# Routing gates scattered into DRAM by accumulating indirect DMAs, searches packed into the first half of the u pass

## The reference

```
q = (xc @ w_q).reshape(TOKEN_CHUNK, PEER_HEADS, 2, PEER_HALF)
s = jnp.einsum('thpd,hpnd->thpn', q, keys)
top_s, top_i = lax.top_k(s, 16)                       # of 128 keys, in each half
cand = top_s[:, :, 0, :, None] + top_s[:, :, 1, None, :]
best_s, best_j = lax.top_k(cand.reshape(..., 256), 16)
expert = i1 * 128 + i2                                # 16384 experts
g = jax.nn.softmax(best_s, axis=-1)
act = gelu(einsum('thk,td->thk', u_tab[expert], xc)) * g
out = einsum('thk,thkd->td', act, v_tab[expert])
```

## Time and profile before

| | |
|---|---|
| median of three runs | 2736.47 us |
| the profiled execution's own time | 2744.57 us |
| its span, first to last instruction | 2742.8 us |
| PE busy | 2465.3 us (90%) |
| DVE busy | 2131.3 us (78%) |
| ACT busy | 1234.8 us (45%) |
| POOL busy | 571.3 us (21%) |
| DMA, mean over the span | 254 GB/s |

### The profile page before, as it was taken

The page is one execution under the profiler, slowest core; times in us unless marked ns, Lnnn a source line. Parts: engine busy times, 40 slices in busy tenths (PEclk is TensorE's granted clock), DMA queues, the critical chain, the costliest instruction groups (busy, mean ns, idle before and its releaser), DMA issues.

```text
span 2742.8 us, 36197 instructions
## 1 busy us (share of the span) xinstructions
PE 2465.3 (90%) x10956; PEld 1938.4 (71%) x10956; DVE 2131.3 (78%) x3891; ACT 1234.8 (45%) x2704; POOL 571.3 (21%) x408
## 2 busy tenths in 40 slices
PE   4987888999899787899999999998878999999996
PEld 3767766666456576777777777776756888878885
DVE  4877613666388855889999999989688888888888
ACT  2332043444312142267777787777433333333333
POOL 2013104422032320011111111112122323232221
PEclk9999999999999899999999999999988999999998
DMA  6646651112032325478888888888899999999996
GB/s 275 217 163 253 255 218 62 62 62 86 23 117 101 146 78 217 136 263 309 322 299 319 298 319 309 305 304 313 318 387 347 381 382 388 384 368 380 389 382 237
DMA packets 223810, 697.60 MB, mean 254 GB/s; under 512 B 15840, under 2 KB 111456, under 8 KB 181472
## 3 DMA queue, kind: packets, MB, share of 16 engines
q1 hardware_dynamic: 165984, 367.25, 37.2%
q0 software_dynamic: 37632, 270.55, 26.0%
q10 hardware_dynamic: 20096, 58.72, 5.6%
HBM read 614.67 MB, written 81.79 MB: 254 GB/s over the span
## 4 chain that ended last, share of the span: by engine, by line
PE 42%; DVE 32%; DVEq 9%; DMA 8%; issue 5%; ACT 3%; SPq 1%; ACTq 1%; POOL 0%; PEldq 0%; PEld 0%
PE ps L866 21%; PE ps L557 7%; DVE g_acc L1787 5%; DVEq L1799 4%; PE ps L542 4%; DVE rows L1778 4%; DVE arena L1454 3%; DMA act_in<-act_scratch 3%; DVE hot L1741 2%; PE ps L569 2%; DMA arena<-in_weights 2%; DVE cand L1397 1%; PE ps L905 1%; DMA rows<-in_rows,pick_e 1%; DMA ring<-in_weights 1%
## 5 line engine op out<-in xcount | busy, mean ns | idle before, releaser
L1999 POOL DMA_INDIRECT rows<-in_rows,pick_e x256 | 333.4, 1302 | 1350.1 <-DVE g_acc L1787 1188.6
L1245 ACT CAST t_hi<-raw 128x1024 fp32r<-128x1024 f32 x256 | 268.8, 1050 | 545.0 <-PE ps L866 528.1
L866 PE MATMUL ps<-t_hi,c_hi 128*128 128x512 f32 x1024 | 407.4, 398 | 37.9 <-DVE t_lo L1859 33.0
L866 PE MATMUL ps<-n_hi,t_hi 128*128 128x512 f32 x1024 | 413.6, 404 | 26.4 <-DVE t_lo L1804 25.3
L866 PE MATMUL ps<-t_lo,c_hi 128*128 128x512 f32 x1024 | 404.4, 395 | 0.0
L866 PE MATMUL ps<-t_hi,c_lo 128*128 128x512 f32 x1024 | 404.1, 395 | 0.0
L866 PE MATMUL ps<-n_hi,t_lo 128*128 128x512 f32 x1024 | 401.2, 392 | 0.0
L866 PE MATMUL ps<-n_lo,t_hi 128*128 128x512 f32 x1024 | 401.0, 392 | 0.0
L1787 DVE SCALAR_TENSOR_TENSOR g_acc<-rows,small,g_acc 128x1024 f32<-128x1024 f32 x254 | 326.3, 1285 | 34.9 <-issue 9.1
L1934 POOL TENSOR_TENSOR w_lo<-ring,w_hi 128x1024 fp32r<-128x1024 f32 x76 | 189.4, 2498 | 667.2 <-ACT w_hi L998 559.9
L866 PEld LDWEIGHTS ps<-t_hi,c_hi 128*128 128x128 f32 x1024 | 196.2, 192 | 85.3 <-issue 44.5
(11 more groups left out here) (198 smaller groups left out, 4188.4 us busy)
## 6 DMA issues: line engine op xcount, KB each, us to landing
raw<-in_table SPq DMA_DIRECT2D x256, 512.0 KB, 7.2
ring<-in_weights SPq DMA_DIRECT2D x44, 2048.0 KB, 8.2
act_scratch<-act_out SPq DMA_DIRECT2D x128, 256.0 KB, 3.5
gate_scratch<-staged ACTq DMA_DIRECT2D x16, 2048.0 KB, 9.7
act_in<-act_scratch SPq DMA_DIRECT2D x128, 256.0 KB, 10.6
gate_in<-gate_scratch SPq DMA_DIRECT2D x32, 1024.0 KB, 15.6
arena<-in_weights ACTq DMA_DIRECT2D x24, 1024.0 KB, 9.4
arena<-in_weights SPq DMA_DIRECT2D x2, 2048.0 KB, 21.2
```

The lines of the kernel that those rows point to most:

```text
L866: last = mm(out, a, b_, start=start and x == 0, stop=stop and x == len(pairs) - 1, skip_group_check=True)
L1245: copy(t_hi[:, t % 2, :], raw[:, t % 4, :]).then_inc(hi_ready, 1)
L1999: G.indirect_dma_start(rows[:, j % 4, :], None, rows_in, bass.IndirectOffsetOnAxis(ap=pick_e[:, j:j + 1], axis=0)).then_inc(row_in[j % 4], 16)
```

## The change

The gate array becomes a DRAM array of cells (one float for each expert and token), laid out so that a tile's 128 x 512 gates are contiguous. SP clears it in the trunk of group 1 by 32 DMAs of 1 MB from a zeroed buffer. After every two searches DVE computes the cell numbers and the softmax weights of 2 x 16 picks for 128 tokens (`place_pair`, `weigh_pair`; ACT does the exp between them), and POOL issues 32 indirect DMAs, 128 single floats each, which add the weights into the cells: 512 in all. The one-hot steps on DVE, ACT and PE, the turned blocks and the 2 MB stores are gone. The v pass loads 256 KB of gates a tile in rows of 2 KB.

The searches all stand in u tiles 0 to 63, half a search a tile; no slots stand there. The slots start at tile 64: two a tile, but one in every fourth, to tile 127 (112 slots, 116 before); in the v pass one a tile and a second one in every eighth (144, 140 before). The v pass of DVE and ACT is written out instead of looped.

```diff
-        gate_dram = scratch("gate_scratch", QUARTERS, P, P, STAGE)
+        gate_cells = scratch("gate_scratch", P * P * SEQS[1], 1)
+        gate_dram = gate_cells.rearrange("(k p t) a -> k p (t a)", p=P, t=SEQS[1])
+        gate_zero = gate_cells.rearrange("(c p m n) a -> c p m (n a)", c=ZEROS, p=P, n=2 * P)
...
         def slots_of(k):
-            if k < 16 or P - 4 <= k < P:
+            if k < DENSE:
                 return ()
-            if k < 4 * CROWDED:
-                return (k - 16,)
...
+            if k < P:
+                j = 2 * (k - DENSE) - (k - DENSE) // 4
+                return (j,) if k % 4 == 3 else (j, j + 1)
+            j = k - 16 + (k - P + 4) // 8
+            return (j, j + 1) if k % 8 == 3 else (j,)
...
         def search_of(k):
-            if k < 4 * SEARCH_BODIES - 2:
+            if k < DENSE:
                 return k // 2, (0, 1) if k % 2 == 0 else (2, 3)
...
+                def clear(c):
+                    sp.dma_start(gate_zero[c], score_in[:, 1].rearrange("p a n -> p (a n)").unsqueeze(1).broadcast_to(
+                        (P, P * P * SEQS[1] // (ZEROS * P * 2 * P), 2 * P))).then_inc(zeroed, 16)
...
             store_act(P - 1)
+            for x in range(4):
+                sp.wait_ge(scattered[x], 16 * TOPK * HEADS)
+            for t in range(4):
+                load_gate(0, t)
...
-            def gate_step(s, parity, taken):
-                pe.wait_ge(sel_copied, taken)
-                pe.wait_ge(hot1_ready, s + 1)
-                pe.wait_ge(hot2g_ready, s + 1)
-                after(pe, g_copied, s - 1)
-                for x in range(4):
-                    last = mm(ps[:, 2 + parity, x * P:(x + 1) * P], hot1[:, parity, x, :], hot2g[:, parity, x, :],
-                              start=True, stop=True)
-                last.then_inc(g_done, 1)
...
+            def place_pair(p):
+                o, n, b = 32 * (p % 2), 32 * p, 2 * (p % 2)
+                keys1, keys2, v = (sel[:, x, o:o + 32] for x in range(3))
+                stt(out=keys1, in0=keys2, scalar=float(P), in1=keys1, op0=ALU.mult, op1=ALU.add)
+                V.tensor_copy(gsum[:, 0:2], v.rearrange("p (h k) -> p h k", k=TOPK)[:, :, 0])
+                dve.drain()
+                tt(v.rearrange("p (h k) -> p h k", k=TOPK), v.rearrange("p (h k) -> p h k", k=TOPK),
+                   gsum[:, 0:2].unsqueeze(2).broadcast_to((P, 2, TOPK)), ALU.subtract).then_inc(pair_shifted, 1)
+                for x in range(2):
+                    ts(cell[:, n + TOPK * x:n + TOPK * (x + 1)], keys1[:, TOPK * x:TOPK * (x + 1)], float(SEQS[1]),
+                       token[:, b + x:b + x + 1], ALU.mult, ALU.add)
...
+            def scatter(s):
+                b = s // TOPK % 4
+                if s % (2 * TOPK) == 0:
+                    pool.wait_ge(pair_ready, s // (2 * TOPK) + 1)
+                if s % TOPK == 0:
+                    after(pool, scattered[b], 16 * TOPK * (s // (4 * TOPK)))
+                G.indirect_dma_start(gate_cells, bass.IndirectOffsetOnAxis(ap=cell[:, s:s + 1], axis=0),
+                                     cell_g[:, s:s + 1], None, compute_op=ALU.add).then_inc(scattered[b], 16)
...
             for k in range(2 * P):
                 for j in slots_of(k):
                     if j + AHEAD < SLOTS:
                         gather(j + AHEAD)
-
-
+                known = 2 * TOPK * sum(pair_of(x) is not None for x in range(min(k, P)))
+                pace = 5 if k < DENSE else 4 if k % 4 == 0 else 3
+                while sent < known and (pace > 0 or k == P - 1):
+                    scatter(sent)
+                    sent += 1
+                    pace -= 1
```

More of the change, by code:

```diff
@@ L375, in load @@
                     load_unit(weights[UNITS_ADA + n], (b + n) % 2)
+                    if g and n == 2:
+                        sp.wait_ge(zero_ready, 1)
+                        for c in range(4):
+                            clear(c)
+                    if g and n in (9, 10):
+                        for c in range(2 * n - 2, 2 * n):
+                            clear(c)
                 if g == 0:
@@ L463, in _ @@
                 load_tile(k + 4)
[L464 to L471, removed]
-                        sp.wait_ge(gates_stored[half], 16 * QUARTERS // 2)
-                    load_gates(0, 0)
+                for x in range(2, SEARCHES):
+                    if starts(x - 1) == k:
+                        load_scores(sp, False, x)
                 if k == P // 2:
@@ L508, in _ @@
                         step(i, t, half)
-                    load_gates(i + 2, half)
             for t in range(4):
@@ L1807, in _ @@
             for k in range(P):
-                i, t = k // 4, k % 4
-                block = (i + 1 - SEARCH_BODIES) // 8 + 2 if (i + 1 - SEARCH_BODIES) % 8 == 0 else None
-                if block is not None and t == 0:
-                    shift_block(block % 2, 1)
-                for s in steps_of(k):
-                    hot_keys(s)
                 lower_tile(k + 1)
@@ L1844, in finish_gathered, with turn @@
                 tt(y, y, f_x1a[:, x, :], ALU.add).then_inc(y_ready, 1)
-            def turn(i, t, half, static=None, last=False):
-                if static is not None:
-                    slots = slots_of(static)
-                    use_slot(slots[0])
-                else:
-                    dve.wait_ge(row_in[t], 16 * i + 16 * (P // 4 + 1))
-                    V.tensor_tensor_reduce(out=rows[:, t, 0:D], in0=rows[:, t, 0:D], in1=x_tok[:, 1, :], scale=1.0,
-                                           scalar=0.0, op0=ALU.mult, op1=ALU.add, accum_out=dot[:, t:t + 1]
-                                           ).then_inc(dotted, 1)
+            def turn(i, t, last=False):
+                slots = slots_of(P + 4 * i + t)
+                use_slot(slots[0])
                 if not (last and t == 3):
@@ L2005, in _ @@
                 gather(j)
+            sent = 0
             for k in range(2 * P):
```

274 lines of the change are left out of this document (85 added, 189 removed).

## The result

The changed kernel takes 3056.64 us (median of four runs, 3051.4 to 3058.72) against 2737.36 us in the four runs of the kernel before beside them: a ratio of 1.1163, 95% interval 1.1144 to 1.1183. The forecast was 2761 us, from 2660 to 2880. The direction was right, the size was not: +319 us instead of +24, outside the range. The profiled execution has a span of 3056.9 us, 314.1 more than the 2742.8 of before.

A forecast was written before the change was run, and what follows sets the result against it. The prediction took DVE, closely followed by PE, to bound the u pass and DMA most of the v pass. It summed 58 - 33 = +25 us, 2770 for the profiled execution, 2761 as median; range 2660 to 2880.

The forecast's parts named there:

- Trunk: Before the u pass: 32 clears of 1 MB on SP's queue cost nothing, at worst up to 15 us.
- Tiles 1 to 64: First half of the u pass: 2.0 us for each of 16 pairs, tile 65 at 1490, 2 us before the old time.
- Tiles 65 to 128: Second half of the u pass: 1.60 us a scatter or gather on POOL, 64 tiles in 531 us.
- The second rival: On POOL an adding scatter is dearer than a gather: at 1.65 us about +125, 2860 us; chance 0.18.
- 8.3 us a tile: Second half of the u pass: time taken as POOL (8.0) and DMA (8.3 to 9.1) press on the same gathers.
- The DMA term: Second half of the u pass: 1.75 gathers and the rest need 6.7 to 7.5 us of DMA a tile, without scatters.
- What a scatter costs DMA: Second half of the u pass: scatters add 0 to 7.5 us of DMA a tile, 1.6 by q1's packets.
- Handover: From u to v pass: first gates wait for the last seven scatters, their landing and a load, 9 us added.
- V pass: First 16 v tiles take about 90 us, 44 less; 11 given back for later tiles: -33, from -50 to 0.
- the average over eight tiles: First 16 v tiles, two second slots among them: DVE needs 41.7 us for eight tiles, PE 44.
- The first: Rival: scatters as short as the shortest gathers, 1.24 us, 6.8 us a tile: -71, about 2665 us; chance 0.33.
- The third: Rival: DVE waits for whole scatters of POOL, 8.7 us a tile in the u pass's second half: +135, 2870; chance 0.04.

## Why the prediction was wrong, step by step

*Trunk: right.* 32 clears cost nothing that shows: tile 2 starts at 1061.29 us, before 1062.96.

*Tiles 1 to 64: right.* Tile 65 at 1482.45 against 1490. A pair costs (1482.45 - 1457.6) / 16 = 1.55 us instead of 2.0.

*Tiles 65 to 128: wrong, and here lies the error.* Two things failed. First the price: 1.60 us for a scatter with its gap, read from the mean gather. Undisturbed it is 1.86, of which the add is 0.58. The first 300 took 1.90 each, and those of the second half 2.10, beyond the upper bound of 1.98: there scatters meet DVE's operations with two inputs. Of the 512 scatters the 204 that met none took at most 1.63 us, the others up to 2.68. The second rival named the reason for the larger part, that an add may cost more.

Second, the place where the price is paid: the sum spread 20 POOL instructions evenly over four tiles, while the list puts 300 scatters ahead of the first gather of this half. The prediction itself worked out that this decides from 1.46 us, and then took 1.60 without applying it. By its own price those scatters would have ended at 1086 + 480 = 1566, a stall of some 80 us that belonged in the forecast, not in a rival of 0.18. At the measured 1.90 the stall is 169 us. Over the whole list, 512 scatters and 112 gathers at 1.60 make 998 us and end at 2084, where the forecast had tile 129 at 2030; in the trace they run from 1083.80 to 2280.60, 1.92 each. So the place was worth some 54 us and the price some 197.

After the stall it took 8.3 us a tile, and 9.74 were needed. In the 594 us of that stage POOL is busy 499.75 and idle 87 between instructions that wait for nothing; 8 remain. So POOL's list, not DMA, is the bound, which the run with six buffers bears out. The DMA term alone was never put to a test: 6.7 to 7.5 us without scatters stand beside 7.09 in the run without any, but that run has four buffers only. That the 8.3 stands near the 8.04 of the run without the add is luck: there POOL's gathers wait 40.5 us for `row_add`, and with six buffers the same work took 7.58.

*What a scatter costs DMA: bounded widely, and small.* In the second half software queue q0 reads, first without scatters, then with 198 plain ones, then with 200 adding ones:

```profile
q0 software_dynamic: 15360, 111.93, 66.3%
```

```profile
q0 software_dynamic: 21678, 112.33, 62.9%
```

```profile
q0 software_dynamic: 44147, 112.38, 59.9%
```

Of 432, 490 and 594 us these are 286, 308 and 356, so an adding scatter takes (356 - 286) / 200 = 0.35 us of all engines and a plain one 0.11: 1.1 and 0.4 us a tile, where 1.6 was taken. These are estimates, as they let the gathers' packets take the same time in all three. An adding scatter is some 144 packets, nine an engine, at about 39 ns. The Trainium skill's "DMA: Bandwidth & Descriptors", section "Bandwidth", gets its 10.5 ns a packet from a transfer of 64 packets in about 0.67 us. The prediction took that for the time of one engine's packet, which the page does not say, so its 0.3 us a tile is not tested by these numbers.

*Handover: 8.3 + 9 = 17.3 us taken for the step from tile 128 to 129, 32.6 measured.* The last t_lo of the u pass stands at 2257.22; POOL then has three gathers and ten scatters left, to 2280.60, and DVE waits for the gates behind them:

```profile
2284.68 1.46 DVE L1643 TENSOR_TENSOR act_in<-act_in,gate_in 128x512 f32<-128x512 f32 x2 [23.72 <-DMA gate_in<-gate_scratch]
```

*V pass: -33 taken, -4 measured.* The first 16 tiles fell to 99.4 us (90 taken), but 11 us were given back for the others, and they took 32. The step that failed is the average over eight tiles, 41.7 us for DVE against PE's 44: with four buffers a second slot makes the next row late, and `row_add` ahead of `c_lo` waits for ACT. The order cost 12 us, the buffers 18 (729.8, 717.8, 700.2). With both mended the average holds: eight tiles take 44.0, and the pass its 700.2, where the prediction's 90 + 598.6 + 11 make 700.

*The rivals.* The second one came about, at 0.18, and its slope of 50 us for each 0.1 from 1.65 would have given 2965 at 1.86; it kept the forecast's handover and the v pass's gain. The first had the price of a plain scatter about right, 1.27 us with its gap, but not even then 6.8 us a tile: 8.04 with four buffers, 7.58 with six. The third, that POOL blocks DVE, did not come about: some 3 us in 64 tiles, and the 234 t_lo that started inside an indirect DMA of POOL took 1.22 us, like the others. That agrees with the row, and not with the rule of the Trainium skill's "SBUF — State Buffer", section "Who interferes with whom", in that direction; in the other it holds, as scatters that met two-input operations of DVE stretched from 1.55 to as much as 2.68 us.

*The range* ended at 2880, where the second rival's price was 1.65, though 1.98 stood as a bound. At 1.98 the list alone gives 300 x 1.98 = 594, a stall of 190 us; the range did not take in the end of its own unknown.

## What to carry to other kernels

When work moves to an in-order queue, add it up in the order of the list, up to each instruction that someone waits for, not as an average over tiles; and put every price through each threshold that you have worked out. An operation that the trace has only in a simpler form (a plain indirect DMA for an adding one) can cost half as much again (1.55 us for 0.97), and more beside other work (1.80), so the range must reach the end of its bound. A second use in one tile costs what it makes late behind it: count buffers and landing time before averaging engines.

## What the runs showed of the hardware

An undisturbed indirect DMA of 128 single floats kept POOL 0.97 us without and 1.55 us with an add, and made some 32 packets ((21678 - 15360) / 198) against 144. Two-input operations of DVE stretched it, up to 2.68 us, and were not stretched by it. A DMA share of 1.00 or more was no ceiling: the same stage moved 388, 398 and 406 GB/s at 1.01 to 1.02, and with 351 instead of 398 GB/s the pass gained 1 of 718 us. PE's granted clock fell from 0.94 to 0.53 where PE was busy 8.73 of 176 us, and stood at 0.83 where PE waited a third of the time; since POOL was the bound, that cost nothing that the runs show.
